# The second block's depthwise convolution as three half-length filters over even and odd tokens

## The chip, the cores and the metric

The kernel runs on one core of one Trainium2 chip. The metric is the device time of one execution in microseconds (us). All arithmetic is in float32; large matrix products are made as three matmuls of a split operand (a high part and a low part), so that TensorE can use its faster operand format fp32r.

## What is computed

Two transformer-like blocks run one after the other on 512 tokens of 1024 features. The change touches one piece of the second block: the branch in which 512 channels of gated projections are convolved over the tokens, each channel with its own 31 taps, then normalised over the channels and passed through a Silu. Around it stand the projections of queries, keys, values and gates, and a stick-breaking attention.

```
def causal_depthwise_conv(u, w, b):            # 31 taps, 512 channels
    y = conv(u padded with 30 zeros in front, w, one group per channel)
    return y + b

proj = h @ w_in
u_val, u_gate = split(proj[:, 0:1024])
u = u_val * sigmoid(u_gate)
u = causal_depthwise_conv(u, conv_w, conv_b)
u = silu(layernorm(u, conv_ln_g, conv_ln_b))
y_conv = u @ w_conv_out
y_att = stick_breaking_attention(q, k, v) @ w_att_out
merged = sigmoid(g_conv) * y_conv + sigmoid(g_att) * y_att
```

## The kernel before

Activations lie with the features on the 128 partitions and the 512 tokens along the free dimension. A weight chunk is 128 x 2048 numbers (1 MB); chunks stream through three slots. SyncE loads chunk c as soon as TensorE has finished chunk c - 3 (L363). ScalarE makes the high part WH (`split_hi`, L448), VectorE the low part WL in the place of the raw chunk (`split_lo`, L947), and TensorE multiplies (L1695 to L1697, three matmuls a product). A half chunk gives one tile of 128 features by 512 tokens in one of eight accumulator banks. Every engine runs its own instructions strictly in the written order and waits on semaphores.

In the second block the order of chunks is: four for u (C_U), two for the keys (C_K2), two for the values (C_V2), two for the queries (C_Q2), eight for the gates, four for the merge. In `tiles_of`, TensorE waits before each chunk for its WL (`have`) and before each tile for its bank: tile i of the value and of the query projection (banks 0 to 3) waits until VectorE has copied the tile of the stage before out of bank i. These copies are k2L (L1459) for the keys, v2F (L1461) for the values, q2L (L1463) for the queries. The values need both of their chunks for every one of the four banks, so the four v2F copies all come behind the second value chunk's preparations in VectorE's order. Query tile 0 waits for v2F number 0. The second scores of the attention wait for the last q2L.

VectorE's order in these three stages is a loop over the stages (L1447). In the key and query stages, ahead of each chunk's two copies, stand a `split_lo` of the chunk after it and a call `conv_taps(9)`. In the value stage stand `split_lo`, `conv_taps(8)`, `split_lo`, `conv_taps(9)`, and then the four copies:

```
if c0 == C_V2 and i == 0:
    for part in range(2):
        split_lo(C_V2 + part + 1)
        conv_taps(8 + part)
elif c0 != C_V2 and n == 0:
    split_lo(c + 1)
    conv_taps(9)
```

One tap of one channel tile (uT holds four tiles k of 128 channels by 512 tokens) is one scalar_tensor_tensor (L1444) that adds tap times shifted uT to cacc; the first tap of a tile is a tensor_scalar (L1441) that also adds the bias. 31 taps of 4 tiles are 124 operations. 53 of them are called in the three projection stages, and 71 in the attention, where `TAPS_AT` says how many belong to pair j of the first twelve of sixteen. In the attention VectorE has to serve TensorE and ScalarE for each pair of heads and query blocks (softplus_sum L1478, softplus_lo L1486, passed_lo L1493), and the taps stand between these. After pair 11 the convolution must be whole: channel sums, mean, variance and root follow, ScalarE applies the Silu (L859) and makes the high part cH (L862), VectorE the low part cL (L1550), and TensorE reads them in the first merge chunk.

Of the kernel before, what the change touches and what calls it, by code (L numbers as in the profile page):

```python
# [19 lines left out]
P = 128  # L20
D, L, LC = 1024, 512, 256
# [10 lines left out]
CT = CW // P  # L32
TAPS = 31
# [45 lines left out]
SP_W = 11 * P  # L79
GATE_ORDER = (*range(12), "mean", 12, 13, "var", 14, 15)  # L80
HALVES = tuple(1 if j in (-1, 5, 10, 16) else 2 for j in range(-1, PAIRS + 1))
TAPS_AT = (2, 7, 4, 10, 5, 5, 7, 8, 5, 5, 7, 6)
GATE_HI_AT, GATE_LO_AT = (-1, 1, 4, 6, 8, 10, 12, 14), (0, 2, 5, 7, 9, 11, 13, 15)
SLOTS = 3
MORE_SLOTS = C_DOWN2 + 2
# [24 lines left out]
U_BANKS = (0, 2, 4, 2)  # L110
BAND = L + (TT - 1) * P
HALF, FOLD = L // 2, L // 2 + 2
# [5 lines left out]
def build(nc, weights, ada, ada_later, x_t, ctx_t, vecs, rope, band, pos, csd, masks, sel, x_rows, gain_row, out):  # L118
    F, R = mybir.dt.float32, mybir.dt.float32r
    ALU, ACT = mybir.AluOpType, mybir.ActivationFunctionType  # L120
    mult, add, sub = ALU.mult, ALU.add, ALU.subtract
    stack = ExitStack()
    with stack:
        KB = 1024
        base = [(nc.sbuf_base + 31) // 32 * 32]

        def fix(name, shape, dt=F):
            size = int(np.prod(shape[1:])) * 4
            t = nc.alloc_sbuf_tensor_at(name, shape, dt, offset=base[0])
            base[0] += (size + 31) // 32 * 32  # L130
            return t

        def over(name, shape, at, dt=F):
            return nc.alloc_sbuf_tensor_at(name, shape, dt, offset=int(at))
# [7 lines left out]
        scratch = fix("scratch", [P, 2, L])  # L142
# [25 lines left out]
        U = base[0]  # L168
# [52 lines left out]
        uT, cacc = over("uT", [P, CT, L], U), over("cacc", [P, CT, L], U + 8 * KB)  # L221
# [11 lines left out]
        xB, gpB = over("xB", [P, 4, L], HALF_AT), over("gpB", [P, D], ACC_AT)  # L233
        mask_in = over("mask_in", [P, 4, P], U + 16 * KB)
        lnsq = over("lnsq", [P, CT, L], U)
        cH, cL = over("cH", [P, CT, L], U, R), over("cL", [P, CT, L], U + 8 * KB, R)
        odd_sq, last_xy, sums = [], [], []
        for m, at in enumerate((U + 88 * KB, U + 88 * KB, U + 16 * KB, U + 88 * KB)):
            odd_sq.append(over(f"odd_sq{m}", [P, 2, L], at))
# [4 lines left out]
        bank = [stack.enter_context(nc.psum_tensor(f"bank{i}", [P, 512], F)) for i in range(8)]  # L244
# [9 lines left out]
        s = Sems()  # L254
# [3 lines left out]
        adaf_in = [stack.enter_context(nc.semaphore(f"adaf{i}_in")) for i in range(ADA_FIRST)]  # L258
        raw_in = [stack.enter_context(nc.semaphore(f"raw{i}_in")) for i in range(SLOTS + 2)]
        ada_in = [stack.enter_context(nc.semaphore(f"ada_half{i}_in")) for i in range(2)]  # L260

        def v(name, i, n=1):
            return vec[:, VAT[name] + i:VAT[name] + i + n]
# [33 lines left out]
        def done(c, n, of):  # L297
            return 16 * c + (n + 1 if n < of - 1 else 16)
# [140 lines left out]
        def _(act):  # L439
            A = nc.scalar.activation  # L440
            own = Chain(act, s.act_own)
# [100 lines left out]
            for d in range(2):  # L542
                for h in range(HEADS):
                    A(zeta[:, d, h, :], v("mpos", d * TC, TC), ACT.Exp,
                      scale=lg[:, 0, d * HEADS + h:d * HEADS + h + 1]).then_inc(s.zeta_exp, 1)
# [42 lines left out]
            for i in range(TT * HEADS):  # L588
                h, j = divmod(i, TT)
# [179 lines left out]
            for c0, ready in ((C_K2, s.k2_hi), (C_V2, None), (C_Q2, s.q2_hi)):  # L769
                for i in range(4):  # L770
                    c, n = c0 + i // 2, i % 2
# [11 lines left out]
            def gate_copy(i):  # L783
                act.wait_ge(s.mm_done, gate_done(i))
                A(gate_buf(i), bank[6 + GATE_ORDER.index(i) % 2][:, :], ACT.Copy).then_inc(s.copied, 1)
# [70 lines left out]
            act.preload_act_table(ACT.Silu)  # L856
            act.wait_ge(s.ln_mul, CT)
            for k in range(CT):
                A(cacc[:, k, :], cacc[:, k, :], ACT.Silu, scale=v("lng", k), bias=v("lnb", k)).then_inc(s.c_silu, 1)  # L859
            for k in range(CT):  # L860
                act.wait_ge(s.c_silu, k + 1)
                A(cH[:, k, :], cacc[:, k, :], ACT.Copy).then_inc(s.c_hi, 1)  # L862
            gate_copy(15)

            def gate_sigmoids(n):
# [18 lines left out]
            for t in range(FT):  # L884
                j = t % 2
# [54 lines left out]
        def _(dve):  # L940
            V = nc.vector
            TT_, TS, STT = V.tensor_tensor, V.tensor_scalar, V.scalar_tensor_tensor
            own = Chain(dve, s.dve_own)

            def split_lo(c, width=CH):
                dve.wait_ge(s.hi_done, c + 1)
                TT_(lo_of(c, 0, width), raw_of(c, 0, width), hi_of(c, 0, width), sub).then_inc(s.lo_done, 1)  # L947
# [239 lines left out]
            for i in range(TT * HEADS + 1):  # L1187
                h, j = divmod(i, TT)
# [204 lines left out]
            for t in range(FT):  # L1393
                j = t % 2
# [27 lines left out]
            for i in range(4):  # L1422
                if i in (1, 2):
                    split_lo(C_U + i + 2)
                dve.wait_ge(s.gate_sig, i + 1)
                TT_(uT[:, i, :], bank[U_BANKS[i]][:, :], scratch[:, i % 2, :], mult).then_inc(s.bank_free, 2)

            conv_n = [0]

            def conv_taps(count):  # L1430

                for _ in range(count):
                    o = conv_n[0]
                    if o == TAPS * CT:
                        return
                    conv_n[0] += 1
                    shift, k = divmod(o, CT)
                    w = v("cw2", (TAPS - 1 - shift) * CT + k)
                    if shift == 0:
                        dve.wait_ge(s.bank_free, B_K2)  # L1440
                        TS(cacc[:, k, :], uT[:, k, :], w, v("cb2", k), mult, add).then_inc(s.conv_tap, 1)  # L1441
                    else:
                        dve.wait_ge(s.conv_tap, o - 3)
                        STT(cacc[:, k, shift:L], uT[:, k, 0:L - shift], w, cacc[:, k, shift:L], mult, add)\  # L1444
                            .then_inc(s.conv_tap, 1)

            for c0, ready in ((C_K2, s.k2_hi), (C_V2, s.mm_done), (C_Q2, s.q2_hi)):  # L1447
                for i in range(4):
                    c, n = c0 + i // 2, i % 2
                    if c0 == C_V2 and i == 0:  # L1450
                        for part in range(2):
                            split_lo(C_V2 + part + 1)
                            conv_taps(8 + part)
                    elif c0 != C_V2 and n == 0:
                        split_lo(c + 1)
                        conv_taps(9)
                    dve.wait_ge(ready, done(C_V2 + 1, i, 4) if c0 == C_V2 else i + 1)
                    if c0 == C_K2:
                        ins = TT_(k2L[:, i, :], bank[i][:, :], k2H[:, i, :], sub)  # L1459
                    elif c0 == C_V2:  # L1460
                        ins = V.tensor_copy(v2F[:, i, :], bank[i][:, :])  # L1461
                    else:
                        ins = STT(q2L[:, i, :], bank[i][:, :], HD2 ** -0.5, q2H[:, i, :], mult, sub)  # L1463
                    ins.then_inc(s.bank_free, 1)
# [23 lines left out]
            def passed_lo(p):  # L1488

                w, at = P * (p % 4 + 1), sp_at(p)  # L1490
                for e in range(2):
                    dve.wait_ge(s.cum_hi, passed(p) - 1 + e)
                    TT_(spL[:, e, at + P:at + w], spF[p % 2][:, e, P:w], spH[:, e, at + P:at + w], sub)\  # L1493
                        .then_inc(s.cum_lo, 1)
# [17 lines left out]
                        .then_inc(s.ln_part, 1)  # L1512

            for j in range(-1, PAIRS):
                taps = TAPS_AT[j] if 0 <= j < len(TAPS_AT) else 0
                if j in GATE_LO_AT:
                    split_lo(C_GATES + GATE_LO_AT.index(j) + 1)
                    conv_taps(taps - 2)
                else:
                    conv_taps(taps - 3)  # L1520
                if j == 14:
                    channel_sum(lnsq)
                if j == 15:
                    dve.wait_ge(s.head_root, HEADS + 1)
                    for k in range(CT):
                        TT_(cacc[:, k, :], cacc[:, k, :], rstd[:, :], mult).then_inc(s.ln_mul, 1)
                    split_lo(C_MERGE + 1)
                if j + 1 < PAIRS:
                    softplus_sum(j + 1)
                conv_taps(2 if j in GATE_LO_AT else min(taps, 3))  # L1530
                if j % 4 in (1, 2):
                    passed_lo(j)
                if j + 1 < PAIRS:
                    softplus_lo(j + 1)
                if j >= 4 and j % 4 == 0:
                    head_pair(j // 4 - 1)
                if j == 11:

                    assert conv_n[0] == TAPS * CT
                    dve.wait_ge(s.conv_tap, TAPS * CT)  # L1540
                    channel_sum(cacc)
                if j == 12:
                    dve.wait_ge(s.head_stat, HEADS + 1)
                    own.link(TS(rstd[:, :], bank[6][:, :], 1.0 / CW, None, mult))
                    for k in range(CT):
                        TT_(cacc[:, k, :], cacc[:, k, :], rstd[:, :], sub).then_inc(s.ln_center, 1)
            head_pair(3)
            for k in range(CT):
                dve.wait_ge(s.c_hi, k + 1)
                TT_(cL[:, k, :], cacc[:, k, :], cH[:, k, :], sub).then_inc(s.c_lo, 1)  # L1550

            for p in range(4):
                if p < 3:
                    split_lo(C_MERGE + p + 2)
                for x in range(2):
                    n = 2 * p + x
# [22 lines left out]
            for t in range(FT):  # L1579
                j = t % 2  # L1580
# [862 lines left out]
```

## Time and profile before

| | us |
|---|---|
| median of 3 runs | 1334.55 (1334.41 to 1335.78) |
| profiled execution | 1334.96 |
| its span, first to last instruction | 1333.2 |
| TensorE busy in it | 1313.8 |
| VectorE busy | 982.8 |
| ScalarE busy | 554.2 |
| GpSimd busy | 88.2 |

The span is what the trace covers; the execution's own time is 1.8 us longer. TensorE's busy time is that of pipelined matmuls whose ends overlap: a matmul of 512 columns is shown with some 390 ns, and the next one starts about 227 ns after it. Starts are therefore the better measure of its pace. VectorE's instructions overlap a little as well: the next one starts some 0.09 us before the shown end of the one ahead.

### The profile page before, as it was taken

What the parts mean: (1) busy time and instruction counts of PE and PEld (TensorE: products, weight loads), DVE (VectorE), ACT (ScalarE), POOL (GpSimd) and SP (SyncE); (2) the same over time, 40 slices, a digit from 0 to 9 for tenths busy, and PEclk for the clock granted to TensorE, in tenths of its full rate; (3) what the DMA queues carried; (4) which work ended last, traced back from release to release, by engine and by line L of the source; (5) the groups of instructions that cost most, each with busy time, mean ns of one, the idle gap of its engine ahead of it and who ended that gap; (6) DMA issues with size and microseconds to landing.
All of it is one profiled execution on the core that took longest, in us unless ns stands there. A gap on an engine that the chain in (4) does not pass through costs nothing.

```text
span 1333.2 us, 15857 instructions
## 1 busy us (share of the span) xinstructions
PE 1313.8 (99%) x6443; PEld 1065.8 (80%) x6443; DVE 982.8 (74%) x1218; ACT 554.2 (42%) x770; POOL 88.2 (7%) x153
## 2 busy tenths in 40 slices
PE   7999999999999999999999999999999999999997
PEld 4799688888888888888888777778878888888885
DVE  4787877999778777677759799866795444346988
ACT  4553444344333343222332566774443222224543
POOL 0000000000001000100000011000002210000001
PEclk9999999999999999999999999999999999999999
DMA  9544055325455546654222211122204333325565
GB/s 387 199 133 137 2 172 199 129 87 187 158 174 179 182 162 207 222 201 164 92 99 95 95 64 48 49 95 95 95 32 158 117 120 103 104 103 195 189 221 190
DMA packets 34473, 188.03 MB, mean 141 GB/s; under 512 B 4304, under 2 KB 5088, under 8 KB 18016
## 3 DMA queue, kind: packets, MB, share of 16 engines
q1 hardware_dynamic: 20976, 140.32, 29.7%
q0 software_dynamic: 13424, 46.69, 10.8%
q8 instruction: 51, 0.84, 0.2%
q14 instruction: 22, 0.18, 0.0%
HBM read 182.79 MB, written 4.20 MB: 140 GB/s over the span
## 4 chain that ended last, share of the span: by engine, by line
PE 84%; DVE 8%; ACT 3%; DMA 3%; issue 2%; SPq 0%; DVEq 0%; ACTq 0%
PE bank L1695 25%; PE bank L1697 24%; PE bank L1696 24%; DVE WL L947 2%; PE bank L2039 2%; PE bank L2040 2%; PE bank L2045 2%; DMA raw<-weights 1%; DMA adaf<-ada 1%; PE bank L1900 1%; DVE ada_acc L989 1%; PE bank L2235 1%; ACT WH L448 1%; PE bank L2205 1%; DVE raw L960 1%
## 5 line engine op out<-in xcount | busy, mean ns | idle before, releaser
L1695 PE MATMUL bank<-hH,WH 128*128 128x512 f32 x992 | 390.1, 393 | 0.9 <-DVE WL L947 0.5
L1697 PE MATMUL bank<-hH,WL 128*128 128x512 f32 x992 | 386.4, 390 | 0.0
L1696 PE MATMUL bank<-hL,WH 128*128 128x512 f32 x992 | 386.3, 389 | 0.0
L947 DVE TENSOR_TENSOR WL<-raw,WH 128x2048 fp32r<-128x2048 f32 (+1 forms) x114 | 253.6, 2227 | 153.8 <-ACT WH L448 153.7
L448 ACT ACTIVATE WH<-raw 128x2048 fp32r<-128x2048 f32 (+1 forms) x117 | 218.0, 1866 | 237.1 <-DMA raw<-weights 179.5
L1695 PEld LDWEIGHTS bank<-hH,WH 128*128 128x128 f32 x992 | 186.3, 188 | 42.5 <-issue 3.3
L1697 PEld LDWEIGHTS bank<-hH,WL 128*128 128x128 f32 x992 | 186.2, 188 | 39.4
L1696 PEld LDWEIGHTS bank<-hL,WH 128*128 128x128 f32 x992 | 186.4, 188 | 37.7 <-issue 0.2
L989 DVE SCALAR_TENSOR_TENSOR ada_acc<-ada_half,csil,ada_acc 128x1024 f32<-128x1024 f32 x70 | 89.7, 1281 | 4.9 <-DMA ada_half<-ada_later 2.3
L1444 DVE SCALAR_TENSOR_TENSOR cacc<-uT,vec,cacc 128x511 f32<-128x511 f32 (+29 forms) x120 | 83.3, 756 | 0.0
L401 POOL DMA_DIRECT2D ada_half<-ada_later x80 | 42.6, 532 | 569.7 <-DVE ada_acc L989 334.9
L1695 PE MATMUL bank<-GH,WH 128*128 128x512 f32 x176 | 68.7, 390 | 0.0
L1697 PE MATMUL bank<-GH,WL 128*128 128x512 f32 x176 | 68.5, 389 | 0.0
L1696 PE MATMUL bank<-GL,WH 128*128 128x512 f32 x176 | 68.5, 389 | 0.0
L1695 PE MATMUL bank<-WH,gH 128*128 128x512 f32 x154 | 60.2, 391 | 2.0 <-DVE WL L947 1.4
L1696 PE MATMUL bank<-WL,gH 128*128 128x512 f32 x154 | 59.9, 389 | 0.0
L1697 PE MATMUL bank<-WH,gL 128*128 128x512 f32 x154 | 59.9, 389 | 0.0
L1402 DVE SCALAR_TENSOR_TENSOR tB<-bank,vec,tB 128x504 f32<-128x504 f32 x22 | 16.4, 743 | 40.8 <-ACT tB L747 40.7
L747 ACT ACTIVATE tB<-bank,vec 128x512 f32<-128x512 f32 x22 | 17.1, 779 | 67.0 <-PE bank L1697 67.0
L894 ACT ACTIVATE gH<-gF 128x1024 fp32r<-128x1024 f32 x11 | 11.7, 1061 | 65.7 <-DVE gF L1602 65.7
L754 ACT ACTIVATE GH<-tB 128x512 fp32r<-128x512 f32 x22 | 14.0, 634 | 59.4 <-DVE tB L1411 59.4
L1697 PEld LDWEIGHTS bank<-GH,WL 128*128 128x128 f32 x176 | 33.0, 188 | 6.9
(360 smaller groups left out, 2176.8 us busy)
## 6 DMA issues: line engine op xcount, KB each, us to landing
raw<-weights SPq DMA_DIRECT2D x119, 1024.0 KB, 5.0
ada_half<-ada_later POOLq DMA_DIRECT2D x80, 512.0 KB, 4.5
adaf<-ada SPq DMA_DIRECT2D x8, 1024.0 KB, 19.8
xT<-x_t SPq DMA_DIRECT2D x4, 512.0 KB, 6.0
x_rows<-xB POOLq DMA_DIRECT2D x32, 64.0 KB, 2.2
gF<-x_rows POOLq DMA_DIRECT2D x3, 512.0 KB, 6.9
ctxT<-ctx_t SPq DMA_DIRECT2D x1, 1024.0 KB, 28.0
out_t<-gF SPq DMA_DIRECT2D x2, 512.0 KB, 2.6
```

The source lines that it names most:

```text
L401: pool.dma_start(ada_half[:, a % 2, :], ada_later[a]).then_inc(ada_in[a % 2], 16)
L448: A(hi_of(c, 0, width), raw_of(c, 0, width), ACT.Copy).then_inc(s.hi_done, 1)
L747: A(tmp[:, j, :], bank[2 * (t % 3) + x][:, :], ACT.Identity, bias=v("cb", x * FT + t), scale=v("cw", 2 * FT + x * FT + t)).then_inc(s.conv ...
L947: TT_(lo_of(c, 0, width), raw_of(c, 0, width), hi_of(c, 0, width), sub).then_inc(s.lo_done, 1)
L989: ins = STT(ada_acc[:, :], w, c_col, ada_acc[:, :], mult, add)
L1444: STT(cacc[:, k, shift:L], uT[:, k, 0:L - shift], w, cacc[:, k, shift:L], mult, add)\
L1695: mm(o, lh, rh, start=start, stop=False, skip_group_check=skip)
L1696: mm(o, lh, rl, start=False, stop=False, skip_group_check=skip)
L1697: return mm(o, ll, rh, start=False, stop=stop, skip_group_check=skip)
L2039: mm(o, wh, hH[:, k, :], start=(k == 0), stop=False)
L2040: mm(o, wl, hH[:, k, :], start=False, stop=False)
L2045: ins = mm(bank[banks[j] + x][:, :], wh, hL[:, k, :], start=False, stop=(k == KT - 1))
```

## The change

A convolution over tokens is split by the parity of the token. With e and o the even and the odd tokens, A the 16 even taps and B the 15 odd taps, the even outputs are A(e) plus B(o) moved by one, and the odd outputs are A(o) + B(e) = (A+B)(e+o) - A(e) - B(o). So three filters of half length are enough: A over e (16 operations), B over o (15), and A+B over e+o (16), with three more operations that form e+o, the difference that the last filter starts from, and the even outputs. That is 50 operations a channel tile, 200 in all, each on at most 256 columns.

For this, uT is written with the even tokens in front and the odd ones behind; two small additions make the taps of A+B and twice the bias in the vector table, behind the last uT and each waited for. The first 144 operations are called in the three projection stages, in six sets of 24, and 56 in the attention, by the new table `CONV_AT`. The Silu of ScalarE puts the tokens back in their order and writes to a tile of its own, cF, from which cH and cL are then made. Work of TensorE, GpSimd and the DMA queues is the same.

```
-TAPS_AT = (2, 7, 4, 10, 5, 5, 7, 8, 5, 5, 7, 6)
+CONV_AT = (3, 5, 3, 7, 4, 4, 5, 6, 4, 4, 6, 5)
+EVEN_TAPS, ODD_TAPS = (TAPS + 1) // 2, TAPS // 2
+CONV_OPS = 2 * EVEN_TAPS + ODD_TAPS + 3
...
-                A(cacc[:, k, :], cacc[:, k, :], ACT.Silu, scale=v("lng", k), bias=v("lnb", k)).then_inc(s.c_silu, 1)
+                A(by_parity(cF[:, k, :]), cacc[:, k, :].rearrange("p (e n) -> p e n", e=2), ACT.Silu, scale=v("lng", k), bias=v("lnb", k)).then_inc(s.c_silu, 1)
...
-                A(cH[:, k, :], cacc[:, k, :], ACT.Copy).then_inc(s.c_hi, 1)
+                A(cH[:, k, :], cF[:, k, :], ACT.Copy).then_inc(s.c_hi, 1)
...
-                TT_(uT[:, i, :], bank[U_BANKS[i]][:, :], scratch[:, i % 2, :], mult).then_inc(s.bank_free, 2)
+                TT_(uT[:, i, :].rearrange("p (e n) -> p e n", e=2), by_parity(bank[U_BANKS[i]][:, :]),
+                    by_parity(scratch[:, i % 2, :]), mult).then_inc(s.bank_free, 2)
+            pairs = v("cw2", CT, 2 * ODD_TAPS * CT).rearrange("p (m e k) -> p m e k", e=2, k=CT)
+            own.link(TT_(v("cw", 0, ODD_TAPS * CT).rearrange("p (m k) -> p m k", k=CT), pairs[:, :, 0, :],
+                         pairs[:, :, 1, :], add))
+            own.link(TT_(v("cw", ODD_TAPS * CT, CT), v("cb2", 0, CT), v("cb2", 0, CT), add))
...
+            def conv_step(n, k):
...
+                even, odd = uT[:, k, 0:HALF], uT[:, k, HALF:L]
+                p_sum, q_sum = cacc[:, k, 0:HALF], cacc[:, k, HALF:L]
...
+                def tap(shift):
+                    return v("cw2", (TAPS - 1 - shift) * CT + k)
...
+                if n < EVEN_TAPS:
+                    if n == 0:
+                        return TS(p_sum, even, tap(0), v("cb2", k), mult, add)
+                    return STT(cacc[:, k, n:HALF], uT[:, k, 0:HALF - n], tap(2 * n), cacc[:, k, n:HALF], mult, add)
+                n -= EVEN_TAPS
+                if n < ODD_TAPS:
+                    if n == 0:
+                        return TS(q_sum, odd, tap(1), None, mult)
+                    return STT(cacc[:, k, HALF + n:L], uT[:, k, HALF:L - n], tap(2 * n + 1),
+                               cacc[:, k, HALF + n:L], mult, add)
+                n -= ODD_TAPS
+                if n == 0:
+                    return TT_(even, even, odd, add)
+                if n == 1:
+                    return STT(odd, p_sum, v("cw", ODD_TAPS * CT + k), q_sum, sub, add)
+                if n == 2:
+                    return TT_(cacc[:, k, 1:HALF], cacc[:, k, 1:HALF], cacc[:, k, HALF:L - 1], add)
+                n -= 3
+                w = v("cw", (ODD_TAPS - 1 - n) * CT + k) if n < ODD_TAPS else tap(TAPS - 1)
+                if n == 0:
+                    return STT(q_sum, even, w, odd, mult, sub)
+                return STT(cacc[:, k, HALF + n:L], uT[:, k, 0:HALF - n], w, cacc[:, k, HALF + n:L], mult, add)
...
-                            conv_taps(8 + part)
+                            conv_taps(24)
...
-                        conv_taps(9)
+                        conv_taps(24)
...
-                TT_(cL[:, k, :], cacc[:, k, :], cH[:, k, :], sub).then_inc(s.c_lo, 1)
+                TT_(cL[:, k, :], cF[:, k, :], cH[:, k, :], sub).then_inc(s.c_lo, 1)
```

What this does to VectorE's order is seen in its list of instructions. First the stretch from the last key copies to the value copies (k2L and v2F are the copies out of the banks, WL is a `split_lo`, cacc is a tap). Before:

```order
L1459 TENSOR_TENSOR k2L<-bank,k2H 128x512 x2
L947 TENSOR_TENSOR WL<-raw,WH 128x2048
L1444 SCALAR_TENSOR_TENSOR cacc<-uT,vec,cacc 128x508 x2
L1444 SCALAR_TENSOR_TENSOR cacc<-uT,vec,cacc 128x507 x4
L1444 SCALAR_TENSOR_TENSOR cacc<-uT,vec,cacc 128x506 x2
L947 TENSOR_TENSOR WL<-raw,WH 128x2048
L1444 SCALAR_TENSOR_TENSOR cacc<-uT,vec,cacc 128x506 x2
L1444 SCALAR_TENSOR_TENSOR cacc<-uT,vec,cacc 128x505 x4
L1444 SCALAR_TENSOR_TENSOR cacc<-uT,vec,cacc 128x504 x3
L1461 COPY v2F<-bank 128x512 x4
```

In the changed kernel the last part of the same stretch, from the second WL on, reads:

```order
L954 TENSOR_TENSOR WL<-raw,WH 128x2048
L1460 SCALAR_TENSOR_TENSOR cacc<-uT,vec,cacc 128x254 x4
L1460 SCALAR_TENSOR_TENSOR cacc<-uT,vec,cacc 128x253 x4
L1460 SCALAR_TENSOR_TENSOR cacc<-uT,vec,cacc 128x252 x4
L1460 SCALAR_TENSOR_TENSOR cacc<-uT,vec,cacc 128x251 x4
L1460 SCALAR_TENSOR_TENSOR cacc<-uT,vec,cacc 128x250 x4
L1460 SCALAR_TENSOR_TENSOR cacc<-uT,vec,cacc 128x249 x4
L1505 COPY v2F<-bank 128x512 x4
```

Where 9 long operations stood between the WL and the copies, 24 short ones stand now, and likewise at the other five places.

In the attention, VectorE's rows around the first pairs (spF is the softplus sum of a pair, spL its low part) were before:

```order
L1478 SCALAR_TENSOR_TENSOR spF_184<-bank,scratch 128x256 x2
L1444 SCALAR_TENSOR_TENSOR cacc<-uT,vec,cacc 128x499 x2
L1486 TENSOR_TENSOR spL<-spF_184,spH 128x256 x2
L1444 SCALAR_TENSOR_TENSOR cacc<-uT,vec,cacc 128x499
L1444 SCALAR_TENSOR_TENSOR cacc<-uT,vec,cacc 128x498 x3
L1478 SCALAR_TENSOR_TENSOR spF_183<-bank,scratch 128x384 x2
```

and are now:

```order
L1522 SCALAR_TENSOR_TENSOR spF_184<-bank,scratch 128x256 x2
L1473 SCALAR_TENSOR_TENSOR cacc<-uT,vec,cacc 128x254 x3
L1530 TENSOR_TENSOR spL<-spF_184,spH 128x256 x2
L1522 SCALAR_TENSOR_TENSOR spF_183<-bank,scratch 128x384 x2
L1473 SCALAR_TENSOR_TENSOR cacc<-uT,vec,cacc 128x254
L1473 SCALAR_TENSOR_TENSOR cacc<-uT,vec,cacc 128x253 x4
```

Fewer taps stand there and each is half as long; the serving operations keep their places among each other.

## Rows read from the trace of the kernel before

**Rows 1.** the page's busy times: us busy (share of the span) x instructions

```profile
PE 1313.8 (99%) x6443; PEld 1065.8 (80%) x6443; DVE 982.8 (74%) x1218; ACT 554.2 (42%) x770; POOL 88.2 (7%) x153
```

**Rows 2.** stretches: us, busy us of each engine (x count), PEclk, DMA share, GB/s

```profile
703.30:714.20 10.90, 10.90 (x49) 9.01 (x48) 9.54 (x13) 4.33 (x3) 0.00 (x0) 1.00 0.27 97
714.20:725.10 10.90, 10.90 (x50) 9.02 (x49) 9.22 (x13) 1.93 (x1) 0.00 (x0) 1.00 0.28 98
725.10:736.00 10.90, 10.90 (x50) 9.03 (x49) 9.37 (x12) 0.60 (x1) 0.00 (x0) 1.00 0.29 96
736.00:746.90 10.90, 10.90 (x49) 8.79 (x47) 8.99 (x12) 3.00 (x3) 0.00 (x0) 1.00 0.28 98
746.90:883.60 136.70, 136.59 (x701) 102.17 (x701) 117.80 (x188) 99.03 (x217) 15.10 (x16) 1.00 0.18 62
```

**Rows 3.** the same stretches for the tap line L1444 alone: us, VectorE busy (x count)

```profile
714.20:725.10 10.90, 5.99 (x9) 1.00 0.28 98
...
746.90:883.60 136.70, 50.62 (x71) 1.00 0.18 62
```

**Rows 4.** VectorE's timeline: start us, us, line, operation, out<-in, shape, count [idle before <-releaser]

```profile
684.72 2.29 DVE L947 TENSOR_TENSOR WL<-raw,WH 128x2048 fp32r<-128x2048 f32 x1 [1.56 <-ACT WH L448]
686.93 1.91 DVE L1441 TENSOR_SCALAR cacc<-uT,vec 128x512 f32<-128x512 f32 x4
...
703.22 0.69 DVE L1459 TENSOR_TENSOR k2L<-bank,k2H 128x512 fp32r<-128x512 f32 x1
...
705.96 2.29 DVE L947 TENSOR_TENSOR WL<-raw,WH 128x2048 fp32r<-128x2048 f32 x1 [1.11 <-ACT WH L448]
...
713.43 2.28 DVE L947 TENSOR_TENSOR WL<-raw,WH 128x2048 fp32r<-128x2048 f32 x1
715.63 5.99 DVE L1444 SCALAR_TENSOR_TENSOR cacc<-uT,vec,cacc 128x506 f32<-128x506 f32 x9
721.53 1.88 DVE L1461 COPY v2F<-bank 128x512 f32<-128x512 f32 x3
```

**Rows 5.** TensorE's timeline at the first matmul of a projection, and of the second scores

```profile
703.33 0.39 PE L1695 MATMUL bank<-WH,hH 128*128 128x512 f32 x1
...
725.09 0.39 PE L1695 MATMUL bank<-hH,WH 128*128 128x512 f32 x1
...
751.01 0.39 PE L2205 MATMUL bank<-q2H,k2H 64*128 64x256 f32 x2
```

**Rows 6.** VectorE's groups by shape (xcount | busy us, mean ns), L1346's own answer, and its timeline

```profile
L1486 DVE TENSOR_TENSOR spL<-spF,spH 128x256 fp32r<-128x256 f32 x8 | 3.0, 421 | 2.4 <-ACT spH L809 2.4
...
L1444 DVE SCALAR_TENSOR_TENSOR cacc<-uT,vec,cacc 128x511 f32<-128x511 f32 x4 | 2.7, 744 | 0.0
...
L1444 DVE SCALAR_TENSOR_TENSOR cacc<-uT,vec,cacc 128x482 f32<-128x482 f32 x4 | 2.7, 716 | 0.0
...
L1346 DVE SCALAR_TENSOR_TENSOR tmp<-xT,gm,bank x6: 474/478/480, 269.3 to 977.1; 128x256 f32<-128x256 f32 x6
...
636.28 0.87 DVE L1346 SCALAR_TENSOR_TENSOR tmp<-xT,gm,bank 128x256 f32<-128x256 f32 x2 [0.37 <-PE bank L1748]
```

**Rows 7.** TensorE's last matmul, and stretches behind it with the granted clock (PEclk)

```profile
1325.08 0.39 PE L1697 MATMUL bank<-WH,gL 128*128 128x512 f32 x1
...
1328.00:1329.00 1.00, 0.00 (x0) 0.00 (x0) 1.00 (x2) 0.20 (x1) 0.00 (x0) 1.00 1.08 383
1329.00:1330.00 1.00, 0.00 (x0) 0.00 (x0) 1.00 (x2) 0.00 (x0) 0.00 (x0) 0.72 0.33 135
1330.00:1331.00 1.00, 0.00 (x0) 0.00 (x0) 0.16 (x1) 0.00 (x0) 0.00 (x0) 0.50 1.01 412
```

**Rows 8.** timeline at the merge: the ScalarE Silu, VectorE's low parts, TensorE's first read

```profile
879.04 2.94 ACT L859 ACTIVATE cacc<-cacc,vec 128x512 f32<-128x512 f32 x4
...
882.53 2.50 DVE L1550 TENSOR_TENSOR cL<-cacc,cH 128x512 fp32r<-128x512 f32 x4
...
889.09 0.39 PE L1695 MATMUL bank<-cH,WH 128*128 128x512 f32 x1
```

More of the change, by code:

```diff
@@ L235, in build @@
         lnsq = over("lnsq", [P, CT, L], U)
-        cH, cL = over("cH", [P, CT, L], U, R), over("cL", [P, CT, L], U + 8 * KB, R)
+        cF = over("cF", [P, CT, L], U)
+        cH, cL = over("cH", [P, CT, L], U + 8 * KB, R), over("cL", [P, CT, L], U, R)
         odd_sq, last_xy, sums = [], [], []
@@ L260, in build, with by_parity @@
         ada_in = [stack.enter_context(nc.semaphore(f"ada_half{i}_in")) for i in range(2)]
+        def by_parity(ap):
+            return ap.rearrange("p (n e) -> p e n", e=2)
         def v(name, i, n=1):
@@ L1425, in _ @@
                 dve.wait_ge(s.gate_sig, i + 1)
-                TT_(uT[:, i, :], bank[U_BANKS[i]][:, :], scratch[:, i % 2, :], mult).then_inc(s.bank_free, 2)
+                TT_(uT[:, i, :].rearrange("p (e n) -> p e n", e=2), by_parity(bank[U_BANKS[i]][:, :]),
[4 more added lines that the diff above has]
+            own.link(TT_(v("cw", ODD_TAPS * CT, CT), v("cb2", 0, CT), v("cb2", 0, CT), add))
+            conv_n = [0]
+            def conv_step(n, k):
[25 more added lines that the diff above has]
+                return STT(cacc[:, k, HALF + n:L], uT[:, k, 0:HALF - n], w, cacc[:, k, HALF + n:L], mult, add)
             conv_n = [0]
@@ L1433, in conv_taps @@
                     o = conv_n[0]
-                    if o == TAPS * CT:
+                    if o == CONV_OPS * CT:
                         return
                     conv_n[0] += 1
-                    shift, k = divmod(o, CT)
-                    w = v("cw2", (TAPS - 1 - shift) * CT + k)
-                    if shift == 0:
+                    n, k = divmod(o, CT)
+                    if n == 0:
                         dve.wait_ge(s.bank_free, B_K2)
-                        TS(cacc[:, k, :], uT[:, k, :], w, v("cb2", k), mult, add).then_inc(s.conv_tap, 1)
                     else:
                         dve.wait_ge(s.conv_tap, o - 3)
-                        STT(cacc[:, k, shift:L], uT[:, k, 0:L - shift], w, cacc[:, k, shift:L], mult, add)\
-                            .then_inc(s.conv_tap, 1)
+                    conv_step(n, k).then_inc(s.conv_tap, 1)
             for c0, ready in ((C_K2, s.k2_hi), (C_V2, s.mm_done), (C_Q2, s.q2_hi)):
@@ L1514, in _ @@
             for j in range(-1, PAIRS):
-                taps = TAPS_AT[j] if 0 <= j < len(TAPS_AT) else 0
+                taps = CONV_AT[j] if 0 <= j < len(CONV_AT) else 0
                 if j in GATE_LO_AT:
                     split_lo(C_GATES + GATE_LO_AT.index(j) + 1)
-                    conv_taps(taps - 2)
+                    conv_taps(taps - 3)
                 else:
-                    conv_taps(taps - 3)
+                    conv_taps(taps - 5)
                 if j == 14:
@@ L1529, in _ @@
                     softplus_sum(j + 1)
-                conv_taps(2 if j in GATE_LO_AT else min(taps, 3))
+                conv_taps(3 if j in GATE_LO_AT else min(taps, 5))
                 if j % 4 in (1, 2):
@@ L1537, in _ @@
                 if j == 11:
-                    assert conv_n[0] == TAPS * CT
-                    dve.wait_ge(s.conv_tap, TAPS * CT)
+                    assert conv_n[0] == CONV_OPS * CT
+                    dve.wait_ge(s.conv_tap, CONV_OPS * CT)
                     channel_sum(cacc)
```

## The prediction

> **What bounds the kernel now.** I read four views, in this order. The page's busy times say that TensorE works 99% of the span [rows 1]. The table of stretches, cut where the second block's projections begin and end, says how evenly that holds in the part that is changed: TensorE is busy for the whole of every 10.9 us chunk of the key, value and query projections, and idle for 0.11 us of the 136.7 us of attention (136.59 busy) [rows 2]. So nothing that only frees VectorE here can shorten the kernel by more than about 0.1 us; what the change can do is make TensorE wait. The same table shows VectorE's load: 9.54, 9.22, 9.37 and 8.99 us of a 10.9 us chunk, which leaves 1.4 to 1.9 us per chunk, and 117.8 of 136.7 us in attention. VectorE's own timeline shows what its time holds [rows 4]: a weight chunk's low half (WL), a set of taps, then the copies that free TensorE's banks. The deadlines are on TensorE's timeline [rows 5]: the value projection begins at 703.33 and the query projection at 725.09. That is two chunks, so a chunk takes 10.88 us and a half chunk (a tile) 5.44.
>
> **The price of a half tap.** Before, one tap is a scalar_tensor_tensor over 482 to 511 columns; nine take 5.99 us from the first start to the last end [rows 4], which at 0.74 for the last [rows 6] is 0.656 us from start to start. The change needs three filters of half length: 50 operations a channel tile, 200 in all, against 124. If an operation cost only its columns, 256 of them would cost half. The rows say otherwise: 511 columns take 744 ns and 482 take 716, about 0.97 ns a column, so the length explains some 500 ns of the 744 and the rest is paid once per operation [rows 6]. The one operation of the same kind at 256 columns (scalar_tensor_tensor with a per-partition scalar, L1346) takes 0.87 us for two in a row at 0.478 each, so 0.39 from start to start [rows 6]. From the long taps by their slope I get 0.66 - 255 x 0.97 ns = 0.41. The two-operand operation on 256 columns (L1486) takes 0.421 us at its end, and two-operand ones start about 0.085 us before the one ahead ends, so 0.335. I take 0.39, falling to 0.38 at 241 columns, since L1346 is the same kind at the same size, and keep 0.335 and 0.41 as ends. The opening operation of a filter is a tensor_scalar: four of 512 columns take 1.91 us [rows 4]; for 256 I take 0.32 (bounds 0.23, half of it, and 0.39).
> The Trainium skill, VectorE: DVE Perf Modes, section on the errata of SBUF-source operations, states 58 cycles plus one per column at 0.96 GHz, 0.327 us for 256 columns. This case's row for the same kind is dearer (0.39). What the page's figure would make of the time stands with the third rival.
>
> **The key, value and query stages.** The six sets were 9, 9, 8, 9, 9, 9 taps and become six of 24. The first four, up to the value copies: 4 x 0.32 + 20 x 0.39 = 9.1; 24 x 0.387 = 9.3; 4 x 0.32 + 20 x 0.382 = 8.9; 24 x 0.39 = 9.4. Together 36.7 us, where 35 taps (4 cheap, 31 at 0.656) took 22.2. VectorE gets 14.5 us more before the value copies and had about 1.5 us a chunk to spare. Step by step, with 2.2 us for a WL, 0.6 for a bank copy (0.69 until its result is there) [rows 4]:
> the first set begins at 686.93 [rows 4], ends at 696.0; two key copies, 697.2; WL of the first value chunk, 699.4; second set, 708.7; third key copy done at 709.4. TensorE's third value tile writes that bank; it is due at 703.33 + 2 x 2.72 = 708.77 (a tile is 2.72 here, since one chunk gives half the sum of four tiles). **TensorE waits 0.65 us.** After the fourth copy, at 709.9, comes WL of the second value chunk, until 712.1 (due at 714.2 + 0.65, in time); third set, 721.0; WL of the first query chunk, 723.2 (due 725.74, in time); fourth set, 732.6; the first value copy is done at 733.3. The first query tile writes the bank which that copy frees, and is due at 725.09 + 0.65 = 725.74. **TensorE waits 7.6 us.** Before, the first three value copies were made from 721.53 [rows 4] and this wait did not exist. Behind the late copy on VectorE stand the other three copies and the next WL, all early enough for a TensorE that starts at 733.3: copies to 735.0, WL 737.2 (due 744.2), fifth set 746.5, two query copies 747.7, WL of the first gate chunk 749.9 (due 755.1), sixth set 8.9, 758.8, last query copy 760.1. TensorE's second scores (bank 2) wait for that copy; they stand 751.01 - 725.09 = 25.9 us behind the start of the query projection [rows 5], so they are due at 759.2. **0.9 us more, if TensorE's clock stays up.**
>
> **What a long wait does to the clock.** At the end of the kernel TensorE's last matmul starts at 1325.08, and the granted clock, 1.00 until then, is 1.00 in 1328 to 1329 and 0.72 in 1329 to 1330: it fell to 0.5 (from 2.4 to 1.2 GHz) about 4 us after TensorE's last work [rows 7]. A wait of 7.6 us is longer, so I expect the query projection to start at 1.2 GHz. No row shows how long it would then stay there. At half clock a matmul of 0.227 us takes 0.453. Bounds: nothing lost, and one whole tile of 24 matmuls at half clock, 24 x 0.227 = 5.4 us. I take 2.0, below the middle, because dense matmuls follow. Since TensorE then comes to the second scores at 761.2, after 760.1, the 0.9 us wait is gone.
> The Trainium skill, TensorE: Matmul & The Clock Gate, Part 1, says the same in kind: an idle stretch puts the array to half clock, and only sustained work releases it. By that rule the clock term is above nothing, which the end of this trace supports.
>
> **Attention.** 71 taps at about 0.64 us (50.62 us busy for them [rows 3]) become 56 at 0.385, 21.6 us. VectorE gains some 24 us there, and TensorE had waited 0.11 [rows 2]: gain 0.1, at most 0.4. The freed time hides no new wait, since VectorE has caught up by 760.1 plus its first softplus pieces. **Edits at nothing:** the two small sums of weights (60 and 4 columns, each waited for) stand where VectorE idled 1.56 us before the WL at 684.72 [rows 4]; nearest operation, 32 columns, 0.18 us, so below 0.6 for both. The even/odd reading of the bank when uT is made costs the same columns; if it doubled, 0.6 us of the same idle 1.56 cover it. The Silu that puts tokens back in order writes with a stride: four take 2.94 us, and the low parts follow at 882.53 for 2.50, until 885.0; TensorE reads them at 889.09 [rows 8]. Even doubled (+2.9) they are there at 888. No DMA is moved or added; the weight loads wait for TensorE's chunks and shift with it.
>
> **The sum.** 0.65 + 7.6 + 2.0 - 0.1 = 10.15 us. On the profiled execution (1334.96 us, span 1333.2) that gives 1345.1; it lay 0.4 above the median of 1334.55, so against the median I predict 1344.7.
>
> **Rivals.**
> 1. *The clock does not fall, or costs nothing.* For it: the trace of before never shows a fall and a rise with work on both sides. Against: the fall at its end. Time: 0.65 + 7.6 + 0.9 - 0.1 = 9.05, 1343.6. Chance 0.17.
> 2. *The clock stays low for a whole tile.* 0.65 + 7.6 + 5.4 - 0.1 = 13.6, 1348.1. Chance 0.12.
> 3. *A half tap costs 0.335 us*, like a two-operand operation (L1486). Every set is then 8.0 us: the third key copy is done at 707.1 (no wait), the first value copy at 728.7, a wait of 3.6 us, too short for the clock. +3.5, 1338.1. Against: L1346. Chance 0.06. By the skill's 0.327 us (VectorE: DVE Perf Modes) the sets are 7.85, the wait 3.0, and the time 1337.4.
> 4. *Not slower: the half taps fit.* One mechanism: if VectorE makes its value copy by 725.09, no bank is late. It has 725.09 - 686.93 = 38.2 us, less four key copies (2.4), three WL (6.6) and the value copy (0.7): 28.5 us for 96 operations, 0.297 us each. At or below that price TensorE never waits, attention gives its 0.1, and the time is 1334.4; up to 0.325 us it stays within 2.7 us of before. Nothing at 256 columns in the trace is that cheap. Chance 0.04 (0.01 of it for more than 0.2% faster, which TensorE's 0.11 us of idle time all but excludes).
> That the change does not do what it says is not open: the order of instructions shows the 200 operations where the words put them.
>
> **How the numbers follow.** My forecast has 0.59; something else that makes it slower (a price of 0.41, which adds 1.8 us to the waits, or a late WL) 0.02. The range must hold 8 in 10: it takes in rivals 1 and 2 with 1.5 us below rival 1 for a price of 0.375 and leaves out rivals 3 and 4, 1342.0 to 1348.5. A measurement of this kernel tells 0.2% (2.7 us) from no change. Slower by more: 0.59 + 0.17 + 0.12 + 0.06 + 0.02 = 0.96, of which I give 0.01 to the third rival coming out under 2.7 us: 0.95. Same 0.04, faster 0.01.
>
> **What would show it.** In the profile of after: half taps at 0.47 to 0.49 us each and 0.38 to 0.39 apart; VectorE busy without a gap from 684 to 760; TensorE waiting once for a value copy (v2F), about 7.6 us from about 725.7, and for a key copy under 1 us near 708.8; the granted clock under 1.00 just behind the long wait; everything after 760 as before but 10 us later, with VectorE idle a quarter of attention. If the wait stands elsewhere (at a WL), my order of deadlines is wrong; if the half taps are at or below 0.30, the whole sum is.

## The result

| | median us | runs | ratio to the kernel before, 95% interval |
|---|---|---|---|
| kernel before | 1334.65 | 1334.41 to 1335.78 (6) | |
| changed kernel | 1346.30 | 1344.02 to 1347.77 (6) | 1.0081 (1.0071 to 1.0091) |
| changed kernel again, another chip, 1334.73 before | 1344.85 | 1343.99 to 1346.49 (5) | 1.0078 (1.0064 to 1.0092) |

The kernel became 10 to 12 us slower. 1344.7 had been forecast, within 1342.0 to 1348.5. The profiled execution took 1344.02 us with a span of 1341.9, 8.7 longer than before.

TensorE's waits of the changed kernel between 640 and 900 us (engine, line waited for: us in total, times, longest); the kernel before has none in the same stretch:

```profile
PE bank L1739 <- DVE v2F L1505: 7.2, 1, 7.2
PE bank L1739 <- DVE k2L L1503: 0.7, 1, 0.7
```

These are the two waits of the prediction. The same table of stretches as [rows 2], and the clock around the long wait (us, TensorE busy, weight loads, VectorE, ScalarE, GpSimd, PEclk, DMA share, GB/s):

```profile
703.30:714.20 10.90, 10.23 (x45) 8.18 (x44) 10.90 (x23) 4.29 (x3) 0.00 (x0) 1.00 0.29 97
714.20:725.10 10.90, 10.90 (x49) 9.01 (x48) 10.90 (x26) 1.92 (x1) 0.00 (x0) 1.00 0.29 98
725.10:736.00 10.90, 3.67 (x11) 2.65 (x10) 10.90 (x24) 0.00 (x0) 0.00 (x0) 0.70 0.29 97
736.00:746.90 10.90, 10.90 (x49) 8.97 (x48) 10.90 (x27) 1.67 (x3) 0.00 (x0) 0.99 0.05 7
746.90:892.00 145.10, 144.97 (x739) 108.85 (x738) 103.71 (x197) 99.49 (x216) 11.34 (x16) 1.00 0.19 65
```
```profile
728.00:729.00 1.00, 0.00 (x0) 0.00 (x0) 1.00 (x4) 0.00 (x0) 0.00 (x0) 1.00 0.80 336
729.00:730.00 1.00, 0.00 (x0) 0.00 (x0) 1.00 (x4) 0.00 (x0) 0.00 (x0) 0.73 1.14 483
730.00:731.00 1.00, 0.00 (x0) 0.00 (x0) 1.00 (x4) 0.00 (x0) 0.00 (x0) 0.50 0.20 82
```

VectorE, 9.0 to 9.5 us busy in a chunk of 10.9 before, is now busy for all of it. TensorE has 3.67 us of work between 725.1 and 736. The granted clock falls to 0.50 (1.2 GHz) at about 729.5, 3.9 us behind the start of the last matmul before the wait. In attention VectorE is down to 103.71 of 145.1 us, and TensorE idles as little as before, 0.13 us. VectorE's own timeline, against [rows 4]:

```profile
686.74 1.37 DVE L1454 TENSOR_SCALAR cacc<-uT,vec 128x256 f32<-128x256 f32 x4
688.03 7.95 DVE L1455 SCALAR_TENSOR_TENSOR cacc<-uT,vec,cacc 128x255 f32<-128x255 f32 x20
695.89 1.29 DVE L1503 TENSOR_TENSOR k2L<-bank,k2H 128x512 fp32r<-128x512 f32 x2
...
708.58 1.30 DVE L1503 TENSOR_TENSOR k2L<-bank,k2H 128x512 fp32r<-128x512 f32 x2
...
722.92 9.51 DVE L1460 SCALAR_TENSOR_TENSOR cacc<-uT,vec,cacc 128x254 f32<-128x254 f32 x24
732.31 2.51 DVE L1505 COPY v2F<-bank 128x512 f32<-128x512 f32 x4
```

Twenty operations of 255 to 251 columns take 7.95 us, 0.393 from start to start. The value copies begin at 732.31, where three of them had begun at 721.53 [rows 4]. TensorE's timeline around the waits, against [rows 5]:

```profile
709.34 0.50 PE L1739 MATMUL bank<-WH,hH 128*128 128x512 f32 x1 [0.67 <-DVE k2L L1503]
```
```profile
725.56 0.39 PE L1741 MATMUL bank<-WH,hL 128*128 128x512 f32 x1
```
```profile
733.18 0.77 PE L1739 MATMUL bank<-hH,WH 128*128 128x512 f32 x1 [7.23 <-DVE v2F L1505]
733.74 0.63 PE L1740 MATMUL bank<-hL,WH 128*128 128x512 f32 x1
734.17 0.63 PE L1741 MATMUL bank<-hH,WL 128*128 128x512 f32 x1
...
736.30 0.39 PE L1740 MATMUL bank<-hL,WH 128*128 128x512 f32 x1
736.53 0.40 PE L1741 MATMUL bank<-hH,WL 128*128 128x512 f32 x1
```

From 733.74 to 736.30 a matmul starts every 0.43 us, the pace of 1.2 GHz, and then every 0.23. Put start against start of the same matmuls before and after, the delay grows by 1.0 us at the key copy, by 7.4 at the value copy and by 1.5 under the low clock, and by 0.3 elsewhere. A clean measure of the part that is changed is the way from TensorE's last matmul of the first block's down projection to its first one on cH: 251.5 us before (637.6 to 889.1), 261.7 after (637.1 to 898.8), +10.2 us. The span grew by 1.5 us less: the changed kernel began this part 0.5 us earlier, and at the end one weight load took 5.3 us where it had taken 6.2, in front of a chain of VectorE. The edit touches neither place; what made them differ is not shown.

### The profile page after: what moved, and what is told of

Its sections match the earlier page's. It is cut to its first block, busy times and chain, and to the rows that moved or that the text cites. A ratio compares the mean times of both kernels' runs of the same rounds, so it can differ in the third digit from the quotient of the medians.

```text
span 1341.9 us, 15936 instructions
## 1 busy us (share of the span) xinstructions
PE 1316.3 (98%) x6443; PEld 1067.0 (80%) x6443; DVE 978.4 (73%) x1296; ACT 554.2 (41%) x770; POOL 84.2 (6%) x153
## 4 chain that ended last, share of the span: by engine, by line
PE 80%; DVE 12%; ACT 3%; DMA 3%; issue 1%; SPq 0%; DVEq 0%; ACTq 0%
PE bank L1739 23%; PE bank L1740 23%; PE bank L1741 23%; DVE WL L954 3%; DVE cacc L1455 2%; PE bank L2083 2%; PE bank L2084 2%; PE bank L2089 2%; DMA raw<-weights 1%; PE bank L1944 1%; ACT WH L455 1%; DMA adaf<-ada 1%; DVE ada_acc L996 1%; PE bank L2279 1%; DVE cacc L1460 1%
## 5 line engine op out<-in xcount | busy, mean ns | idle before, releaser
L1740 PEld LDWEIGHTS bank<-GL,WH 128*128 128x128 f32 x176 | 33.0, 188 | 6.8
L1739 PEld LDWEIGHTS bank<-GH,WH 128*128 128x128 f32 x176 | 33.0, 188 | 6.8
```

Of the source, the lines that this page charges most:

```text
L1739: mm(o, lh, rh, start=start, stop=False, skip_group_check=skip)
L1740: mm(o, lh, rl, start=False, stop=False, skip_group_check=skip)
```

## The experiments

Some of the texts below name the theory in short: VectorE holds too much work ahead of the value copies. "Stretch" is the 251.5 us from above, read from each kernel's own trace.

**Fewer half-length operations in the projection stages.** The sets hold 16, 20 and 22 operations in place of 24, and the attention takes the rest; the arithmetic is the same.

```
-                            conv_taps(24)
+                            conv_taps(16)
...
-                        conv_taps(24)
+                        conv_taps(16)
...
-CONV_AT = (3, 5, 3, 7, 4, 4, 5, 6, 4, 4, 6, 5)
+CONV_AT = (6, 10, 6, 13, 8, 7, 9, 11, 7, 7, 11, 9)
```

> Edit of the changed kernel: the six sets of half-length operations in the key, value and query stages hold 16 instead of 24; 104 of the 200 stand in the attention. Theory (VectorE is overfilled ahead of the value copies): four sets take 4 x 8 x 0.39 = 12.5 us less, the first value copy is possible before 725, TensorE waits neither for k2L nor for v2F, the clock stays up, and the time is that of the kernel before, 1334 to 1335.5 us. The attention takes 104 x 0.385 = 40 us of taps where the kernel before had 45, so no wait there. Rival (the half-length form itself costs TensorE time, by its count of operations or semaphores): the time stays near 1346, whatever the place of the operations.

> As sets16 with 20 operations in each set (120 of 200), 80 in the attention. Theory: four sets take 6.2 us less than with 24, the first value copy's result is there at 733.2 - 6.2 = 727.0, 2.0 us after TensorE is due (725.0); the stall is about 2.0 us, too short for the clock to fall (4 us), and the time is 1336.3 to 1337. Rival (any wait behind a copy lowers the clock): 1 to 5 us more.

> As sets16 with 22 operations in each set (132 of 200), 68 in the attention. Theory: first value copy at 730.1, stall about 4.9 to 5.1 us, just longer than the 4 us after which the granted clock fell: 1339.6 if the clock holds, 1341 to 1344 if it falls, with a spread of runs of some us in the second case. Rival (the load counts only as a total): no difference between this, sets20 and the changed kernel.

| operations in a set | median us | ratio (interval) | TensorE's wait for v2F | stretch against before |
|---|---|---|---|---|
| 16 | 1334.61 | 0.9998 (0.9989 to 1.0006) | none | 0.0 |
| 20 | 1338.85 | 1.0026 (1.0015 to 1.0036) | 1.9 | +3.8 |
| 22 | 1342.36 | 1.0055 (1.0039 to 1.0071) | 5.1 | +8.0 |
| 24 | 1346.30, 1344.85 | 1.0081, 1.0078 | 7.2 | +10.2, +10.0 |

The table of stretches of the kernel with sets of 16 (columns as in [rows 2]):

```profile
703.30:714.20 10.90, 10.90 (x50) 9.03 (x49) 9.79 (x20) 4.32 (x3) 0.00 (x0) 1.00 0.28 97
714.20:725.10 10.90, 10.90 (x50) 9.03 (x49) 10.32 (x21) 1.92 (x1) 0.00 (x0) 1.00 0.28 98
746.90:883.60 136.70, 136.59 (x701) 102.19 (x701) 112.91 (x222) 99.07 (x217) 14.10 (x16) 1.00 0.18 62
```

VectorE again has idle time in every chunk (9.79 and 10.32 us busy of 10.9), and TensorE is back at 136.59 us in attention, to the hundredth what it had been [rows 2]. So the half-length form by itself costs nothing and gains nothing beyond the 0.1% that the interval leaves: the place of the operations decides. The waits follow the forecast (2.0 and 4.9 to 5.1 us expected, 1.9 and 5.1 found). The time with sets of 20 does not: 1336.3 to 1337 had been expected, because a wait of 2 us was taken to be too short for the clock. Its trace, TensorE's timeline and the clock:

```profile
725.94 0.39 PE L1741 MATMUL bank<-WH,hL 128*128 128x512 f32 x1
728.27 0.47 PE L1739 MATMUL bank<-hH,WH 128*128 128x512 f32 x1 [1.94 <-DVE v2F L1505]
...
729.50 0.39 PE L1741 MATMUL bank<-hH,WL 128*128 128x512 f32 x1
729.73 0.58 PE L1739 MATMUL bank<-hH,WH 128*128 128x512 f32 x1
730.11 0.63 PE L1740 MATMUL bank<-hL,WH 128*128 128x512 f32 x1
```
```profile
729.00:730.00 1.00, 1.00 (x5) 0.83 (x4) 1.00 (x3) 0.00 (x0) 0.00 (x0) 0.89 0.96 393
730.00:731.00 1.00, 1.00 (x4) 0.71 (x4) 1.00 (x1) 0.00 (x0) 0.00 (x0) 0.50 0.43 180
```

The clock fell 1.5 us after TensorE had gone back to work, and stayed low for eight matmuls; the delay against before grew by 1.6 us over them. So the rival's point was right here: a short wait can lower the clock, and 1338.85 is within the 1 to 5 us more that it gave. The kernel's ten runs lie between 1336.09, with a mean clock of 0.999, and 1340.97, with 0.997. Only one of them has a trace, and the runs of the kernel before, which has no such wait, show the same mean clocks (0.995 to 0.999), so in how many of the ten the clock fell is not shown.

With sets of 22 the clock falls within the wait (0.64 from 728 to 729, where TensorE has no work), and 1342.36 us lies in the 1341 to 1344 expected for that case. The spread of some us that was expected with it did not come: its four runs lie within 0.7 us.

**Long taps in the same overload.** The kernel before, with 14 of its own full-length taps in a set and 40 in the attention.

```
-TAPS_AT = (2, 7, 4, 10, 5, 5, 7, 8, 5, 5, 7, 6)
+TAPS_AT = (2, 4, 2, 5, 3, 3, 4, 5, 3, 3, 4, 2)
...
-                            conv_taps(8 + part)
+                            conv_taps(14)
...
-                        conv_taps(9)
+                        conv_taps(14)
```

> Edit of the kernel before: its own full-length taps, but 14 in each of the six sets (84 of 124 in the key, value and query stages, 40 in the attention). Theory (time of VectorE's work in front of the value copies decides, not the form): a set takes 14 x 0.655 = 9.2 us, as 24 half-length operations do; the first value copy is there at about 732.4, TensorE waits about 7.4 us, the clock falls, and the time is 1343 to 1347 us. Rival (it is the half-length form or its longer list of operations that costs): 1335 us.

1343.32 us (1.0067, 1.0052 to 1.0082), stretch +9.3. TensorE's waits in it from 700 to 780, and VectorE's fourth set:

```profile
PE bank L1695 <- DVE v2F L1461: 7.3, 1, 7.3
```
```profile
723.03 9.19 DVE L1444 SCALAR_TENSOR_TENSOR cacc<-uT,vec,cacc 128x502 f32<-128x502 f32 x14
732.14 2.48 DVE L1461 COPY v2F<-bank 128x512 f32<-128x512 f32 x4
```

9.2 us of long taps do what 9.4 us of half-length ones do. The microseconds of VectorE's work in front of the copies are the cause; the form and the number of instructions are not. (The key copy is not late here, and the stretch is 0.9 us shorter than that of the changed kernel.)

**Value copies ahead of the fourth set.** The changed kernel, with the fourth set behind the value copies.

```
-                            conv_taps(24)
+                            if part == 0:
+                                conv_taps(24)
...
                         ins = V.tensor_copy(v2F[:, i, :], bank[i][:, :])
+                        if i == 3:
+                            ins.then_inc(s.bank_free, 1)
+                            conv_taps(24)
+                            continue
```

> The changed kernel with the fourth set of 24 moved from in front of the four value copies to behind them. Theory (the three stages together hold more VectorE work than TensorE's time): the wait for the value copy goes, but what is behind it comes late: the low halves of the second query chunk and of the first gate chunk by about 1.5 and 1.9 us, and the second scores by about 6 us, because the last query copy comes at 761; 1344.5 us, more if the clock falls. Rival (only the order in front of the value copies is wrong): one wait of 0.7 us is left, 1335.5 us.

1346.75 us (1.0093, 1.0076 to 1.0110), stretch +12.7. TensorE's waits from 700 to 780:

```profile
PE bank L2254 <- DVE q2L L1512: 6.3, 1, 6.3
PE bank L1744 <- DVE WL L954: 2.7, 2, 1.5
PE bank L1744 <- DVE k2L L1504: 0.7, 1, 0.7
```

The wait for the value copy is gone, and the three waits named in the expectation stand in its place: both low halves (1.5 and 1.9 expected, 2.7 together), the last query copy (6.0 expected). From the first matmul behind the last wait until the clock is back, the delay grows by another 2.3 us; 1344.5 had been given for a clock that holds. This reordering moves the wait and does not pay it: the three stages hold more VectorE work than TensorE gives time for.

**The price of the per-partition tap.** The changed kernel with a constant in its place, so that the convolution's values are not the reference's.

```
-                    return STT(cacc[:, k, n:HALF], uT[:, k, 0:HALF - n], tap(2 * n), cacc[:, k, n:HALF], mult, add)
+                    return STT(cacc[:, k, n:HALF], uT[:, k, 0:HALF - n], 0.5, cacc[:, k, n:HALF], mult, add)
```

(and so in the other four scalar_tensor_tensor calls of `conv_step`)

> The changed kernel with the constant 0.5 in place of the per-partition tap in every scalar_tensor_tensor of the convolution: the convolution's values are left out, all else is the same. Theory (0.06 us of each half-length operation is the per-partition scalar): start to start 0.335 instead of 0.393 us, four sets 5.1 us shorter, the wait for the value copy 3.1 us, no fall of the clock, 1337.6 us. Rival (the scalar's form costs nothing): 1346 us.

1338.60 us (1.0031, 1.0020 to 1.0041), stretch +3.1. Its first and fourth set, and TensorE's wait:

```profile
688.01 6.73 DVE L1455 SCALAR_TENSOR_TENSOR cacc<-uT,cacc 128x255 f32<-128x255 f32 x20
...
719.03 8.03 DVE L1460 SCALAR_TENSOR_TENSOR cacc<-uT,cacc 128x254 f32<-128x254 f32 x24
```
```profile
PE bank L1739 <- DVE v2F L1505: 2.8, 1, 2.8
```

6.73 us where the changed kernel has 7.95: 0.06 us of each operation's 0.39 is the per-partition scalar. The wait is 2.8 us (3.1 expected). The profiled run shows no low clock behind it, as had been forecast:

```profile
728.00:732.00 4.00, 4.00 (x18) 3.27 (x18) 4.00 (x6) 0.00 (x0) 0.00 (x0) 1.00 0.25 107
```

A wait of 1.9 us was followed by a fall with sets of 20, and this one of 2.8 was not. So the length of the wait alone does not tell whether the clock falls. The profiled run took 1336.84 us; the others, at mean clocks of 0.996 to 0.998, are 0.9 to 3.4 us longer, and without a trace of them the reason is not shown.

**Keeping TensorE busy.** 31 matmuls whose result nobody reads fill the long wait of the changed kernel; 8 fill that of the kernel with sets of 20.

```
+            for n in range(31):
+                mm(bank[6][:, :], hH[:, n % KT, 0:P], hH[:, n % KT, :], start=True, stop=True, skip_group_check=True)
             tiles_of(C_Q2, B_Q2)
```

> The changed kernel with 31 additional matmuls of 512 columns on TensorE between the value and the query projection, into a bank that nobody uses then; they add nothing to the result. 31 x 0.227 = 7.0 us, which fits into the 7.4 us that TensorE waits for the value copy. Theory (the low clock is a cost of its own and is what makes the runs of the changed kernel differ by 3.8 us): the wait is filled, the granted clock stays 1.00, the time is 1334.65 + 0.7 + 7.4 = 1342.7 us, and the runs agree within about 1.5 us. Rival (the spread has another cause, and the clock costs nothing): 1346 us and the same spread as the changed kernel.

> The changed kernel with 31 additional matmuls in the wait, as before, beside the changed kernel on one chip. Theory (the low clock costs 1.5 us and more in some runs, and filling the wait takes that away): 1.5 to 2.5 us below the changed kernel's median, less 0.6 us for the second scores that now wait for the last query copy. Rival (the clock's cost is hidden by that copy or is none): the same median as the changed kernel within 0.5 us.

> The changed kernel itself, unedited, on the same chip and between the same runs of the kernel before as the two that follow, since the traces account for 9.6 us (0.7 + 7.4 of waits, 1.5 of low clock) and the medians of different chips differ by 11.6. If the extra 2 us belong to the kernel, it is at 1345.5 to 1346.5 here too; if they are of that chip, 1344 to 1345.

> Sets of 20 with 8 additional matmuls (1.8 us) in the place of the 1.9 us that TensorE waited there. The trace of sets of 20 showed the clock fall for 3.4 us after that short wait, at a cost of 1.6 us. Theory (the short wait is what made it fall): granted clock 1.00 throughout, 1334.5 + 2.0 = 1336.5 us, 2 us below sets of 20. Rival (the clock fell for another reason): 1338.8 us as there.

| | without | with the filling |
|---|---|---|
| changed kernel, first series (different chips) | 1346.30 | 1344.72 |
| changed kernel, second series (same chip) | 1344.85 | 1344.59 |
| its stretch | +10.2, +10.0 | +9.0, +9.0 |
| sets of 20 (different chips, 1334.66 and 1334.73 before) | 1338.85 | 1337.60 |
| its stretch | +3.8 | +2.8 |

With the filling the clock stays at 1.00, here in the changed kernel:

```profile
730.00:732.00 2.00, 2.00 (x11) 1.65 (x10) 2.00 (x6) 0.00 (x0) 0.00 (x0) 1.00 0.02 8
732.00:734.00 2.00, 1.84 (x9) 1.25 (x8) 2.00 (x5) 0.00 (x0) 0.00 (x0) 1.00 0.00 0
```

and TensorE's waits from 640 to 900 are

```profile
PE bank L1739 <- DVE k2L L1503: 0.7, 1, 0.7
PE bank L2251 <- DVE q2L L1507: 0.6, 1, 0.6
PE bank L1739 <- DVE v2F L1505: 0.2, 1, 0.2
```

A new wait of 0.6 us for the last query copy takes back a part of the 1.5 us that the low clock had cost: TensorE now comes earlier to a copy that VectorE makes no earlier. The traces show the net gain, 1.0 to 1.2 us of the stretch. The medians on the same chip differ by 0.26 us, which runs that spread over 1.6 to 2.5 us can't tell from 1; by the times alone the rival, the same median within 0.5 us, would stand. In the first series the filled kernel came out 2.0 us above its expected 1342.7, and its runs still spread over 2.7 us. So the spread is not the clock's alone, and the theory that said so is not borne out. With sets of 20 the filled kernel's eleven runs lie within 1.7 us and the unfilled one's ten within 4.9; the 1336.5 expected is missed by 1.1. Its trace has a wait that nothing in the edit makes:

```profile
PE bank L1739 <- DVE uT L1433: 0.4, 1, 0.4
```

It lies at 671 us, ahead of all the taps. ScalarE could start the high part of a weight chunk only at 665.95 instead of 665.20, because that chunk's load landed later, and a uT copy of VectorE came late behind it. By the end of the value projection this has added 0.65 us to the stretch, start against start. Without it the filled kernel is 2.2 us above before instead of 2.8, and filling has taken off the whole 1.6 us of the low clock. How late a weight load lands is thus one thing besides the clock that makes runs differ.

**No taps at all.** The kernel before without all but the first tap of each tile, so that the convolution is left out.

```
-                    if o == TAPS * CT:
+                    if o == CT:
```

> The kernel before with all taps but the first of each channel tile left out (4 operations of 124): VectorE has some 80 us less work. Theory (nothing in VectorE's taps holds TensorE up in the kernel before): 1334.2 to 1334.7 us, at most 0.4 us faster; so no cheaper convolution could have gained. Rival (VectorE at 86% in attention costs TensorE something that the trace does not show as a wait): more than 2 us faster.

1334.84 us (1.0003, 0.9994 to 1.0013). VectorE's 117.8 us of busy time in attention are down to 69.94, and TensorE's 136.59 stay as they are:

```profile
746.90:883.60 136.70, 136.59 (x702) 101.90 (x701) 69.94 (x114) 97.70 (x215) 11.15 (x16) 1.00 0.18 62
```

The stretch is even 1.0 us longer, and not by the edit: TensorE has one wait of 0.8 us for a uT copy at 671 us, behind a weight chunk whose high part began 1.45 us later than before. A cheaper convolution on VectorE, whatever its price, could not have made this kernel faster by more than the 0.8 us that the interval leaves.

## Why the prediction was right

- *What bounds the kernel.* "What the change can do is make TensorE wait" held; sets of 16 and the kernel without taps both end at the time of before.
- *The price of a half tap.* 0.39 us from the one operation of the same kind and size; measured 0.393. The opening tensor_scalar: 0.32 estimated, and four take 1.29 us to the next start (1.05 for the four of the second filter, which add no bias). The four sets were to take 36.7 us and took 36.6. The rival's 0.335 was the price of operations without a per-partition scalar, which the constant taps confirm.
- *The wait for the key copy.* 0.65 us expected at 708.77; the matmul came 1.0 us late. The copy ended some 0.2 us later, against TensorE's own time, than worked out, and the first matmul after a wait is followed at 0.34 instead of 0.23 us.
- *The wait for the value copy.* 7.6 us until 733.3 expected, 7.4 us until 733.18 found. Behind it no low half was late, as the list of deadlines said.
- *The clock.* The fall came where the end of the kernel before had put it. The low clock cost 1.5 us where 2.0 had been taken, as a guess, between 0 and 5.4. The clock stayed low through the rest of the wait and rose at about 736.3, after TensorE had worked again from 733.18 on. That agrees with the Trainium skill (TensorE: Matmul & The Clock Gate, Part 1), by which activity is what releases the throttle.
- *The second scores.* With the clock down, no wait for the last query copy had been expected; the delay grows by 0.13 us there. VectorE, expected busy without a gap until 760, waits once, for 0.80 us at 747.5.
- *The edits at nothing.* The two sums of weights take 0.21 and 0.16 us and VectorE still idles 1.31 us behind them. The strided Silu takes 844 ns in place of 800, and TensorE finds the low parts ready.
- *Attention.* 60 operations of 25.3 us in place of 50.6 us, and no gain but noise.
- *The sum* was 10.15 us. The trace accounts for 10.2 in the stretch; the medians say 11.6 and 10.1. That the sum fits to 0.05 is luck: 0.35 too little at the key copy, 0.2 too much at the value copy, 0.5 too much for the clock, and 0.4 too little for the rest (0.1 gained expected, 0.3 lost) cancel. What the first series has beyond the second belongs to that series and not to the kernel, which came out at 1344.85 when run again. Its mean clocks are in part lower (0.993 to 0.996 against 0.995 to 0.996); where the time was lost stays open, since only one run of it has a trace.

One step was wrong, though the sum did not rest on it: the third rival took a wait of 3.6 us to be "too short for the clock", and the expectations of three experiments carried that on. A single fall, seen at the end of a kernel behind 4 us without work, was read as the least that it takes. It only showed a fall behind as much. A wait of 1.9 us was followed by one, and a wait of 2.8 us was not.

## What to carry to other kernels

When work is moved among the stages of an engine that is not the bound, add up its microseconds before each copy that frees a bank, and compare with when the bounding engine comes for it; a lower total (here VectorE is busy for 978.4 us instead of 982.8) is worth nothing if it stands in front of a deadline. An operation's price has a part per instruction, so a form with half the columns and 1.6 times the instructions saves hardly anything: look for a row of the same kind and size, scalars included. And when a copy is late, find out whether another order can help by listing the deadlines behind it too; here three others were waiting.

## What was not expected of the hardware

- TensorE's clock fell after a wait of only 1.9 us, and did so 1.5 us after work had begun again. In the traces with waits of 5 us and more it fell within the wait, and in the one with 2.8 us not at all. A late bank can be paid for twice: the wait, and then matmuls at 0.43 instead of 0.23 us.
- A per-partition scalar costs a scalar_tensor_tensor of 256 columns 0.06 us (0.39 against 0.33 from start to start).
- A Silu that writes every second element takes 844 ns instead of 800 for 512 columns.
